# Second block's stationary tiles moved, gate rows by transposes, norm sums of split squares, unread products turned into transposes

## The reference, cut to what matters

```python
b = cumsum(log_sigmoid(f_pre))                       # per head, over tokens
D[t, s] = b[t] - b[s] + i_pre[s],  s <= t            # needs r[s] = i_pre[s] - b[s] as a row
m_t = max(b[t] + m_prev, max_s D[t, s])
W = exp(D - m_t);  SW = (q k^T) * W
h = SW v / max(|sum_s SW|, exp(-m_t))
h = h * rsqrt(mean(h * h) + eps) * gain              # per head: a norm over 128 features
```

## Time and profile before

| what | value |
|---|---|
| three runs | 881.32, 882.76, 882.77 us; median 882.76 |
| the profiled execution | 881.85 us, span 880.5 us |
| TensorE busy | 868.9 us, 99% of the span |
| DVE, ACT busy | 725.3 us (82%), 571.6 us (65%) |
| TensorE clock granted, mean | 0.997 |

### The profile page before, as it was taken

One profiled execution on the slowest core, in us unless ns is written; L12 is line 12 of the kernel. 1 busy time (PEld: TensorE's weight loads), 2 busy tenths in 40 slices (PEclk: granted clock), 3 DMA queues, 4 the chain that ended last, 5 costly groups with the idle time before them and its releaser, 6 DMA issues.

```text
span 880.5 us, 18440 instructions
## 1 busy us (share of the span) xinstructions
PE 868.9 (99%) x7310; PEld 847.6 (96%) x7310; DVE 725.3 (82%) x1169; ACT 571.6 (65%) x845; POOL 1.9 (0%) x9
## 2 busy tenths in 40 slices
PE   8999999999999999999999999999999999999997
PEld 6999989999999999999999999899999999999996
DVE  6788999899989899888887999988788985555554
ACT  7858466675696787654446879677785664444542
POOL 0000000000000000000000000000000000000000
PEclk9999999999999999999999999999999999999998
DMA  8866456556775789999995576754445666666551
GB/s 304 285 197 232 147 162 195 170 189 212 269 250 187 259 288 335 320 306 331 335 333 168 162 213 211 214 165 126 165 152 178 196 197 193 197 195 197 180 162 48
DMA packets 59045, 189.87 MB, mean 216 GB/s; under 512 B 8640, under 2 KB 11088, under 8 KB 58832
## 3 DMA queue, kind: packets, MB, share of 16 engines
q1 hardware_dynamic: 58816, 188.69, 65.2%
q10 hardware_dynamic: 144, 0.00, 0.0%
HBM read 186.57 MB, written 1.05 MB: 213 GB/s over the span
## 4 chain that ended last, share of the span: by engine, by line
PE 89%; ACT 5%; DVE 4%; issue 1%; DMA 1%; SPq 0%; DVEq 0%; ACTq 0%
PE bank L1084 27%; PE bank L1087 26%; PE bank L1086 26%; ACT whi L2022 2%; PE bank L1057 1%; PE bank L1056 1%; PE bank L1055 1%; DMA H<-in_xT 1%; DVE wlo L1129 1%; PE bank L1018 0%; PE bank L1025 0%; PE bank L1021 0%; DVE mqk L1549 0%; PE bank L884 0%; PE bank L759 0%
## 5 line engine op out<-in xcount | busy, mean ns | idle before, releaser
L1129 DVE TENSOR_TENSOR wlo<-raw,whi 128x1024 fp32r<-128x1024 f32 x291 | 353.5, 1220 | 84.1 <-ACT whi L2022 83.5
L2022 ACT ACTIVATE whi<-raw 128x1024 fp32r<-128x1024 f32 x291 | 304.9, 1056 | 174.5 <-PE bank L1087 169.9
L1084 PE MATMUL bank<-Alo,whi 128*128 128x256 f32 x1328 | 371.2, 280 | 0.0
L1087 PE MATMUL bank<-Ahi,whi 128*128 128x256 f32 x1328 | 367.3, 277 | 0.0
L1086 PE MATMUL bank<-Ahi,wlo 128*128 128x256 f32 x1328 | 367.3, 277 | 0.0
L1084 PEld LDWEIGHTS bank<-Alo,whi 128*128 128x128 f32 x1328 | 249.4, 188 | 2.8 <-issue 2.6
L1086 PEld LDWEIGHTS bank<-Ahi,wlo 128*128 128x128 f32 x1328 | 249.5, 188 | 0.4 <-issue 0.2
L1087 PEld LDWEIGHTS bank<-Ahi,whi 128*128 128x128 f32 x1328 | 249.8, 188 | 0.0
L1087 PE MATMUL bank<-Fhi,whi 128*128 128x256 f32 (+1 forms) x320 | 88.9, 278 | 0.0
L1086 PE MATMUL bank<-Fhi,wlo 128*128 128x256 f32 (+1 forms) x320 | 88.9, 278 | 0.0
L1084 PE MATMUL bank<-Flo,whi 128*128 128x256 f32 x256 | 70.8, 276 | 0.0
(11 more groups left out here) (437 smaller groups left out, 1376.7 us busy)
## 6 DMA issues: line engine op xcount, KB each, us to landing
raw<-in_stream SPq DMA_DIRECT2D x298, 512.0 KB, 4.3
arows<-in_ada SPq DMA_DIRECT2D x64, 384.0 KB, 5.2
TB<-in_TB SPq DMA_DIRECT2D x1, 1536.0 KB, 7.2
a8r<-a SPq DMA_DIRECT2D x16, 64.0 KB, 3.9
out<-H SPq DMA_DIRECT2D x4, 256.0 KB, 2.9
bc<-in_bc SPq DMA_DIRECT2D x1, 896.0 KB, 5.4
H<-in_xT SPq DMA_DIRECT2D x1, 512.0 KB, 7.8
mats<-in_mats SPq DMA_DIRECT2D x1, 449.0 KB, 7.1
```

The lines of the kernel that those rows point to most:

```text
L1084: pe.matmul(os[j], wh, xl, start=k == 0 and (wide or j == 0), stop=False, skip_group_check=not wide)
L1087: i = pe.matmul(os[j], wh, xh, start=False, stop=k == K - 1 if wide else last, skip_group_check=not wide)
L1129: v.tensor_tensor(wlo[:, s % NHL, :], raw[:, s % NRAW, :], whi[:, s % NHL, :].bitcast(F32), ALU.subtract).then_inc(*lo_v.up(s))
L2022: a.activation(whi[:, s % NHL, :], raw[:, s % NRAW, :], ACT.Copy).then_inc(*hi.up(s))
```

## The change

1. The tiles of the second block get new gaps. From the start of `whi`, modulo 512, `aacc`, `av2`, `Wp` and `P3` now all lie at 0, and so do the new `rc2` and `pick`; the new `onesr` lies at 480. `mv` and `ones` stay.
2. Step b: DVE writes the column r twice (columns 0 and 32) into `rc2`, zero elsewhere by a memset of GpSimd. PE transposes it (new step of `ifg` at slab 188), ACT copies the result to the float32r tile `rrow` (high part), DVE writes the low part into rows 32 to 35 (slab 189). The product is now one float32r matmul, with `pick`'s column broadcast as the stationary operand, which adds rows h and 32+h. `diagonals` and its DVE step at slab 188 go.
3. Step n: ACT also writes `nhi`, the squares in float32r, DVE `nlo`, the rest; PE makes two float32r products with `onesr` in place of one in float32. ACT also writes `onesr`.
4. `plain` becomes `turn`, a transpose of the identity. `sums` has none any more; GLA's products get one behind them, and so does the last o step of `att2`.
5. The last o step of `att2` moves by half a slab on PE, its ACT and DVE steps by one slab.

```diff
-    "ifg": ([186], [182, 185, 187], [182, 183]),
+    "ifg": ([186, 188], [182, 185, 187, 189], [182, 183, 188]),
...
-              [188, 192, 194, 198, 201, 202, 204, 204, 207, 210, 213, 213, 214],
+              [192, 194, 198, 201, 202, 204, 204, 207, 210, 213, 213, 214],
...
-    "att2": ([193, 198, 199, 199, 204, 205, 205, 210, 211, 211, 215.5, 217],
-             [194, 196, 200, 200, 201, 206, 206, 208, 212, 212, 213, 218],
-             [194, 198, 199, 200, 204, 205, 206, 210, 211, 212, 215, 217]),
+    "att2": ([193, 198, 199, 199, 204, 205, 205, 210, 211, 211, 215.5, 217.5],
+             [194, 196, 200, 200, 201, 206, 206, 208, 212, 212, 213, 219],
+             [194, 198, 199, 200, 204, 205, 206, 210, 211, 212, 215, 218]),
...
         arows = s2("arows", [128, 4, 768])
+        s2("gap8", [128, 16])
         aacc = s2("aacc", [128, 768])
...
-        s3("gap3", [128, 136])
+        onesr = s3("onesr", [128, 128], F32R)
+        s3("gap3", [128, 8])
...
+        s3("gap5", [128, 64])
         av2 = s3("av2", [128, 2, 512])
-        diag = s3("diag", [128, 2, 2, 128])
+        nhi = s3("nhi", [128, 2, T], F32R)
+        nlo = s3("nlo", [128, 2, T], F32R)
+        rc2 = s3("rc2", [128, 2, 128])
+        rrow = s3("rrow", [128, T], F32R)
+        pick = s3("pick", [128, 4], F32R)
+        s3("gap4", [128, 120])
         Wt = s3("Wt", [128, 2, 384])
         Wp = s3("Wp", [128, 2, 384])
         mst = s3("mst", [128, 2, 16])
+        s3("gap6", [128, 96])
         P3 = s3("P3", [128, 2, 2, 384])
...
-            def plain(b):
-                pe.matmul(banks[b][:, 0:128], ones[:, :], mats[:, 0:128], start=True, stop=True)
+            def turn(b):
+                pe.transpose(banks[b][:, 0:128], ident, ident)
...
                     i.then_inc(*gla_pe.up("c", c))
+                turn(3)
...
                 i.then_inc(*ada_pe.up("turned"))
-                plain(5)
...
+                w.wait_ge(*ifg_v.at("rcol"))
+                for tt in range(2):
+                    i = pe.transpose(b[:, 128 + tt * 128:256 + tt * 128], rc2[:, tt, :], ident)
+                i.then_inc(*ifg_pe.up("rows"))
+                yield
...
-                        w.wait_ge(*ml_v.at("d", hp, i))
-                        w.wait_ge(*(ml_s.at("root", hp - 1, i) if hp else ifg_v.at("bcum")))
-                        pe.matmul(b[:, 0:256], ones[:, :], diag[:, i, :, :], start=True, stop=True
+                        w.wait_ge(*(ml_s.at("root", hp - 1, i) if hp else ifg_v.at("rlo")))
+                        h = 2 * hp + i
+                        pe.matmul(b[:, 0:T], pick[:, h:h + 1].broadcast_to([128, 128]), rrow[:, :], start=True, stop=True
...
-                        w.wait_ge(*ml_s.at("q", hp, i))
                         w.wait_ge(*ml_v.at("hb", hp, i))
-                        pe.matmul(banks[3 + i][:, 0:T], ones[:, :], hsc[:, i, 0, :], start=True, stop=True
+                        w.wait_ge(*ml_v.at("nlo", hp, i))
+                        pe.matmul(banks[3 + i][:, 0:T], onesr[:, :], nhi[:, i, :], start=True, stop=False)
+                        pe.matmul(banks[3 + i][:, 0:T], onesr[:, :], nlo[:, i, :], start=False, stop=True
...
+                    if hp == 3:
+                        turn(5)
...
-                v.tensor_tensor(rcol[:, :, :], ift[:, :, 0:4], bcum[:, :, :], ALU.subtract).then_inc(*ifg_v.up("rcol"))
+                for at in (0, 32):
+                    i = v.tensor_tensor(rc2[:, :, at:at + 4], ift[:, :, 0:4], bcum[:, :, :], ALU.subtract)
+                i.then_inc(*ifg_v.up("rcol"))
+                v.tensor_tensor(pick[:, :], ident[:, 0:4], ident[:, 32:36], ALU.add).then_inc(*ifg_v.up("pick"))
+                yield
+                w.wait_ge(*ifg_s.at("rhi"))
+                v.tensor_tensor(rrow[32:36, :], banks[3][32:36, 128:384], rrow[32:36, :].bitcast(F32), ALU.subtract
+                                ).then_inc(*ifg_v.up("rlo"))
...
-                    if hp == 0:
-                        diagonals(1)
+                    for i in HF:
+                        w.wait_ge(*ml_s.at("nhi", hp, i))
+                        v.tensor_tensor(nlo[:, i, :], hsc[:, i, 0, :], nhi[:, i, :].bitcast(F32), ALU.subtract
...
                 a.activation(lf[:, :, :], lf[:, :, :], ACT.Ln, bias=1.0).then_inc(*ifg_s.up("ln"))
+                a.activation(onesr[:, :], ones[:, :], ACT.Copy).then_inc(*ifg_s.up("ones"))
+                yield
+                w.wait_ge(*ifg_pe.at("rows"))
+                a.activation(rrow[:, :], banks[3][:, 128:384], ACT.Copy).then_inc(*ifg_s.up("rhi"))
...
+                    for i in range(2):
+                        w.wait_ge(*ml_s.at("q", hp, i))
+                        a.activation(nhi[:, i, :], hsc[:, i, 0, :], ACT.Copy).then_inc(*ml_s.up("nhi", hp, i))
...
+            g.memset(rc2[:, :, :], 0.0).then_inc(*mpad_g.up("rc"))
```

More of the change, by code:

```diff
@@ L381, in build @@
         arows = s2("arows", [128, 4, 768])
+        s2("gap8", [128, 16])
         aacc = s2("aacc", [128, 768])
         csil = s2("csil", [128, NADA])
-        s2("gap2", [128, 2048 - 768 - NADA])
+        s2("gap2", [128, 2048 - 768 - NADA - 16])
         Blo = s2("Blo", [128, 2, T], F32R)
@@ L420, in build @@
         mst = s3("mst", [128, 2, 16])
+        s3("gap6", [128, 96])
         P3 = s3("P3", [128, 2, 2, 384])
         stat3 = s3("stat3", [128, 16])
+        s3("gap7", [128, 96])
         p3h = ExitStack()
@@ L627, in tensor_program @@
             w = Waiting(pe)
-            def plain(b):
-                pe.matmul(banks[b][:, 0:128], ones[:, :], mats[:, 0:128], start=True, stop=True)
+            def turn(b):
+                pe.transpose(banks[b][:, 0:128], ident, ident)
             def between():
                 for b in BETWEEN.values():
-                    plain(b)
+                    turn(b)
                     yield
@@ L892, in r4 @@
                 yield
-                plain(7)
+                turn(7)
                 yield
@@ L1566, in ifg_task @@
                 w.wait_ge(*ifg_v.at("bcum"))
-                v.tensor_tensor(rcol[:, :, :], ift[:, :, 0:4], bcum[:, :, :], ALU.subtract).then_inc(*ifg_v.up("rcol"))
+                w.wait_ge(*mpad_g.at("rc"))
+                for at in (0, 32):
[6 more added lines that the diff above has]
+                                ).then_inc(*ifg_v.up("rlo"))
                 yield
@@ L1572, in mlstm @@
                 HF = range(2)
[L1573 to L1584, removed]
                 for hp in range(2):
@@ L1641, in mlstm @@
                         v.tensor_copy(hsc[:, i, 1, :], banks[3 + i][:, 0:T]).then_inc(*ml_v.up("hb", hp, i))
-                    if hp == 0:
-                        diagonals(1)
+                    for i in HF:
+                        w.wait_ge(*ml_s.at("nhi", hp, i))
+                        if hp:
+                            w.wait_ge(*ml_pe.at("n", hp - 1, i))
+                        v.tensor_tensor(nlo[:, i, :], hsc[:, i, 0, :], nhi[:, i, :].bitcast(F32), ALU.subtract
+                                        ).then_inc(*ml_v.up("nlo", hp, i))
                     yield
@@ L2557, in gpsimd_program @@
             g.memset(mpad[:, :, 0:3], 0.0).then_inc(*mpad_g.up("set"))
+            w.wait_ge(*mpad_g.at("set"))
+            g.memset(rc2[:, :, :], 0.0).then_inc(*mpad_g.up("rc"))
         programs = ((sync_program, nc.sync), (tensor_program, nc.tensor), (vector_program, nc.vector),
```

## The result

The changed kernel takes 897.9 us (median of 4 runs, 897.65 to 898.17) against 882.76 us before: the medians are 15.1 us apart, where I had forecast 2.7 us faster, and the ratio is 1.018 (95% interval 1.0169 to 1.0192). The profiled execution has a span of 896.9 us, against 880.5. It ended as the rival "the turn leaves the slow pace" says.

A forecast was written before the change was run, and what follows sets the result against it. TensorE, busy 99% of the span and 89% of the chain, was taken to bound the kernel. Terms -0.26 - 0.31 - 1.11 + 0 - 0.1 - 0.92 = -2.7 us, from 882.76, gave 880.0 us; range 877.8 to 882.8.

The forecast's parts named there:

- the turn leaves the slow pace: Rival: the turn behind `r4` slows 1483 matmuls, +6.5 us, 886.6 us; at slab 68 likewise, +9.7; chance 0.09.
- The step that failed: Premise for moved tiles and turns: a transpose from distance 0 to `whi` (modulo 512) leaves the fast pace; 4.4 ns per matmul.
- Against: Argument against the slow-turn rival: the transposes of `P1`, at distance 0, are followed by the fast pace, 0.1136 us a step.
- the two weak gains: Rivals: paces not set by addresses, 881.6 us, chance 0.18; a new wait not covered, 880.7 to 881.1 us, 0.06.
- Unread products at 40 and 68: Slabs 40 and 68: products of 0.24 us become transposes of 0.11; two turns save 2 x 0.13 = 0.26 us.
- GLA's turn: Behind GLA's products: +0.11 for the transpose, -0.42 for 96 matmuls no longer slow, together -0.31 us.
- `sums`: At `sums`: -0.24 for the removed product, -0.87 for 197 matmuls no longer slow up to 490.86 us; together -1.11.
- 518.49 to 580.16: Stretch where ACT and DVE bound the chain: `onesr` +0.2, DVE -0.25, net 0, bounds -0.3 and +0.3; TensorE's new wait covered.
- First n and second b: 587.81 to 608.83 us: n saves 0.41 and b 0.64, but only -0.1 of 1.05 counts, the rest becoming a wait.
- The end of the attention: Second block's attention: n -0.41, `P3` pace -0.26, o-step wait -0.23, its turn +0.11, `r4`'s turn -0.13; together -0.92 us.
- The clock: Rival: TensorE falls to 1.2 GHz for one slab after each of six turns, 2.7 us each, +16 us; chance 0.01.

The follow-up runs named there:

- the first experiment: Also experiment 1: changed kernel with every turn taken out; unread products back at slabs 40, 68, 183 and behind `r4`, none in GLA or `att2`: 881.86 us, ratio 1.0001.
- experiment 7: Changed kernel without any turn, `aacc` and `P3` back at 448 and 384 bytes from `whi`, product of `sums` still gone: 880.63 us, ratio 0.9992.
- experiment 14: Kernel before with only the product of `sums` removed, `aacc` left where it was: 880.1 us against 881.38, ratio 0.9984.
- experiment 5: Changed kernel with the unread product back at slab 68 alone, all other turns kept: 888.41 us.
- experiment 6: Changed kernel with an unread product at all six places where it has a turn: 880.79 us, ratio to the kernel before 0.9992.
- experiment 12: Changed kernel with two transposes instead of one at slab 68 and behind `r4`: 882.24 us, ratio 0.9995.
- experiment 8: Changed kernel with six transposes of the identity instead of one at slab 68 and behind `r4`: 882.31 us, ratio 1.0011.
- experiment 10: Changed kernel without any turn and with nothing at slab 68 and behind `r4`; unread products at 40 and 183: 881.26 us, ratio 0.9984.
- experiment 11: Changed kernel with unread products instead of turns at slabs 40, 68, 183, behind `att2` and `r4`, none in GLA: 880.48 us, ratio 0.9972.
- experiment 13: Changed kernel with its single transpose read from distance 384 at slab 68 and 256 behind `r4`, other turns kept: 888.14 us.
- experiment 2: Kernel before with only the unread products at slab 68 and behind `r4` made turns: 896.3 us against 881.45, ratio 1.015.
- experiment 9: The kernel of experiment 3 run again unchanged, on another chip; no time given, paces the same in 25 of 25 stretches behind the added work.
- experiment 3: Kernel before with unread transposes and products of several kinds and numbers added every fourth slab of the two long stretches; no time given.

## Why the prediction was wrong, step by step

**The step that failed** is "I take it that a transpose from distance 0 leaves the fast pace, whatever was before." It was drawn from groups of six and applied to a single one. For groups of six from 0 it held for `P3`, `P1`, `aacc` and the identity's columns, in every trace. It did not hold for `Wp`, which the change had moved to 0 as well: 4 of its 20 groups there left the slow pace, two of them in the first experiment. Its second, with 22 steps of 0.1177 us behind it:

```profile
621.49 0.82 PE L850 MATMUL bank<-mats,Wp 128*128 128x128 f32 x6
...
622.26 0.28 PE L1101 MATMUL bank<-Ahi,wlo 128*128 128x256 f32 x1
...
624.85 0.28 PE L1102 MATMUL bank<-Ahi,whi 128*128 128x256 f32 x1
```

For one transpose it failed at the two places that matter, with +9.6 and +6.6 us, which the rival had priced at +9.7 and +6.5 (the time that I gave for it, 886.6, counted the second alone). I gave that rival 0.09, for two reasons that the rows didn't bear out. "Against" it I had set the transposes of `P1`, which are six. And I took the fast pace in the long stretches for the normal one, where it needed the operation that the change takes away: with 3700 matmuls behind two operations, the question was what a small change there could do. A slip in the chances changed nothing: a third of the two weak gains is (0.18 + 0.06) / 3 = 0.08, not 0.06.

*Unread products at 40 and 68,* -0.26: the saving is real (0.08 us from the start of the turn to that of the next matmul, 0.25 for the product), and it drowns. At slab 40 the pace stayed fast.

*GLA's turn,* -0.31: wrong, by the step that failed. The stretch behind it stayed slow and so did the next, where the kernel before is fast. From 93.5 us to slab 68's operation, the turns in GLA and at slab 40 were to save 0.44 us, and it took 0.30 more (124.22 against 123.92).

*`sums`,* -1.11: right in size, -1.05 in the trace and -1.3 when done alone. The reason was half wrong: the product made the slow stretch here, not the place of `aacc` (experiments 7 and 14).

*518.49 to 580.16,* 0: wrong in part. From 499.59 on the chain took 0.47 us more than before, and I had put the bound at 0.3. All of it lies behind the last `lf` entry (before at 541.46 us, after at 550.10): from there to the product it is 39.26 us, before 38.70 (the first part, 50.51 against 50.60, is no longer). The traces tell the parts. Without the new steps it is 38.69 to 38.71 in all seven traces. With them it is 38.96 to 38.98 where the 72 matmuls behind the transposes of `rc2` are fast (experiments 5, 6, 7 and 12) and 39.25 to 39.27 where they are slow (the changed kernel, 1, 8, 10, 11 and 13). So the new steps cost about 0.27, of which `onesr` is 0.21, as I had taken it. The other 0.29 is again the pace, 72 x 0.0044 = 0.32, and it counts because the cover that I relied on failed: I wrote that the chain doesn't pass TensorE before 580.16, and in just these six traces it does, from the transposes on (559.96 to 568.92 above).

*First n and second b,* -0.1: right. What TensorE saves turns into a wait at the second output step, 1.25 us, and from the chain's product at 589.36 to that step it is 28.56 us, before 28.67.

*The end of the attention,* -0.92. Its parts came through: `P3`'s stretches are fast, n is four matmuls, and no wait stands at the last output step. They were given back, and more, by the pace: 324 matmuls behind the turn at 662.51 us slow (+1.4) and 108 behind the scores at 642.67 (+0.5). That is how the -1.0 of this item and the one above became +0.70, and it is why the kernel without turns (experiment 1) gains nothing: the 324 are slow there as well, and fast in experiment 6, at 1.1 us less.

*The clock:* no row has less than 1.00 in the long stretches. The Trainium skill, page "TensorE: Matmul & The Clock Gate", section Part 4: PE-mode transpose, says that a transpose doesn't count as TensorE being busy in the way that a matmul does. No run here shows a lower clock behind transposes: behind single, double and sixfold ones the windows have 1.00, and what changed was the spacing at full clock.

**Open:** what sets the pace. That the two turns carry the loss is shown (experiments 1, 2, 5 and 8); why a turn leaves the slow pace is not. Behind the same side work in the same program the pace mostly repeats (experiment 9), and it follows neither from the kind, the number or the place alone, nor from the pace ahead alone (experiments 3, 10 and 14). It can also come out otherwise in one program: once between the traces of experiments 3 and 9, and it seems in single executions, as the last section tells.

## What to carry to other kernels

Measure the distance of back-to-back matmuls at full clock and look for two values; then find the last side operation ahead of each long stretch, since that one may be worth microseconds (9.6 and 6.6 here). A spacer that looks useless can be what holds the fast pace: price its removal at the whole stretch behind it, with both signs, and try one, two and six of it on the chip. A small gain that rests on the pace is not to be summed with others, since any edit can turn the pace of a stretch behind it.

## What the runs showed of the hardware

- Float32r matmuls of 256 columns run at 113.3 or 117.8 ns each, both at a granted clock of 1.00. One pace lasted over 2184 and 1488 matmuls, and over three products with `ones` in between.
- The restart tells it early: behind the slow one at 217.84 the next starts are 0.20, 0.12 and 0.12 us on, behind the fast ones the third is 0.11.
- Behind the added work, the paces of 25 stretches were the same in two executions of one kernel on two chips; one other stretch, 24 matmuls, came out differently.
- Single executions fell out by about the price of the last stretch: 890.14 among three of 896.1 to 896.6 in experiment 2, 887.7 among eleven of at most 881.63 in experiment 6, and two of the kernel before, 887.61 and 887.96, where the other 95 beside the experiments took at most 883.58. That this is the stretch behind `r4` is argued from 1488 x 0.0044 = 6.5 alone; none of them was profiled.
- The kernel before has two common times, about 881.3 and 882.9 us. On two chips (three sets, 63 runs) most were near the lower, on two others (34 runs) all but four were above 882.2. That gap is about 336 x 0.0044 = 1.5, the stretch behind `att2`'s last output step, but this is a guess: its only trace, at 881.85, has that stretch fast. So a gain of 0.1 or 0.2% is to be read only against runs on the same chip.
- Six transposes of `P3` from 384 bytes past `whi` (modulo 512) left the slow pace 27 times of 28, from 0 the fast one 40 times of 40. Six of `Wp` from 0 left the fast one 16 times of 20, so no rule follows for other tiles.
